# The first half of a ConvFFN's up projection as seven block products, one core of a Trainium2 chip

## What is computed

```
n2 = rmsnorm(h, ln2)
up = n2 @ w_up                                  # 1024 -> 2 * 2816
u, vv = up[..., :D_FF], up[..., D_FF:]
uc, conv_tail = causal_dwconv(u, conv_prev, conv_w, conv_b)   # width 3, along the tokens
h = h + (jax.nn.gelu(uc, approximate=False) * vv) @ w_down
```

## Time and profile before

| | us |
|---|---|
| median of three runs | 832.52 (831.88 to 833.23) |
| span of the profiled execution (first to last instruction) | 830.1 |
| around the span, by the median | 2.4 |
| TensorE busy | 818.1 |
| VectorE busy | 589.9 |
| ScalarE busy | 374.6 |
| GpSimd busy | 219.3 |

### The profile page before, as it was taken

One profiled execution on the slowest core, in us unless ns is written; L12 is line 12 of the kernel. 1 busy time (PEld: TensorE's weight loads), 2 busy tenths in 40 slices (PEclk: granted clock), 3 DMA queues, 4 the chain that ended last, 5 costly groups with the idle time before them and its releaser, 6 DMA issues.

```text
span 830.1 us, 15732 instructions
## 1 busy us (share of the span) xinstructions
PE 818.1 (99%) x6538; PEld 807.0 (97%) x6538; DVE 589.9 (71%) x764; ACT 374.6 (45%) x523; POOL 219.3 (26%) x258
## 2 busy tenths in 40 slices
PE   9999999999999999999999999999999999999996
PEld 8999999999999999999999999999999999999996
DVE  4474668477898886767558877777777756878973
ACT  5553234232354553534343644444444424544574
POOL 4018236434335600000430433333233222000020
PEclk9999999999999999999999999999999999999998
DMA  8769967983324984538899598589699873555522
GB/s 267 219 203 166 269 218 165 193 229 131 108 103 93 208 258 143 164 103 262 147 250 280 88 257 216 157 190 195 248 208 209 222 168 123 180 180 171 175 65 107
DMA packets 167889, 152.27 MB, mean 183 GB/s; under 512 B 6677, under 2 KB 155881, under 8 KB 167804
## 3 DMA queue, kind: packets, MB, share of 16 engines
q1 hardware_dynamic: 121612, 109.73, 42.3%
q0 software_dynamic: 46048, 41.04, 28.9%
q10 hardware_dynamic: 160, 0.53, 0.2%
HBM read 145.31 MB, written 58.40 MB: 245 GB/s over the span
## 4 chain that ended last, share of the span: by engine, by line
PE 92%; DVE 5%; ACT 1%; issue 1%; DMA 0%; DVEq 0%; SPq 0%; ACTq 0%
PE mm L1999 52%; PE ax L2290 14%; PE mm L2404 8%; PE ax L2404 6%; PE ax L2018 6%; PE mm L2290 4%; PE ax L2023 2%; DVE grs L1431 1%; DVE wlo L1421 1%; PE mm L2011 0%; DVE s0g L1588 0%; DVE ylo L1666 0%; PE mm L2018 0%; DVE wlo L1678 0%; ACT whi L1008 0%
## 5 line engine op out<-in xcount | busy, mean ns | idle before, releaser
L1999 PE MATMUL mm<-nhi,whi 128*128 128x272 f32 x960 | 203.2, 293 | 1.2 <-DVE wlo L1421 0.6
L1999 PE MATMUL mm<-nhi,wlo 128*128 128x272 f32 x960 | 199.3, 289 | 0.0
L1999 PE MATMUL mm<-nlo,whi 128*128 128x272 f32 x960 | 198.7, 288 | 0.0
L1008 ACT ACTIVATE whi<-raw 128x1024 fp32r<-128x1024 f32 (+2 forms) x111 | 128.4, 1190 | 67.5 <-PE mm L1999 38.5
L1999 PEld LDWEIGHTS mm<-nhi,whi 128*128 128x128 f32 x960 | 151.9, 189 | 3.8 <-DVE wlo L1421 0.8
L1999 PEld LDWEIGHTS mm<-nlo,whi 128*128 128x128 f32 x960 | 151.3, 189 | 0.0
L1999 PEld LDWEIGHTS mm<-nhi,wlo 128*128 128x128 f32 x960 | 150.8, 190 | 0.0
L1678 DVE TENSOR_TENSOR wlo<-raw,whi 128x1024 fp32r<-128x1024 f32 (+1 forms) x78 | 84.4, 1123 | 5.7 <-ACT whi L1008 3.2
L1421 DVE TENSOR_TENSOR wlo<-raw,whi 128x2048 fp32r<-128x2048 f32 x28 | 67.0, 2394 | 17.8 <-ACT whi L1008 17.8
L939 POOL DMA_DIRECT2D v_sums<-in_w_up x24 | 30.7, 4231 | 117.4 <-DVE mlo L1749 116.6
L1008 ACT ACTIVATE whi<-ring 128x1408 fp32r<-128x1408 f32 x25 | 34.6, 1383 | 44.1 <-PE ax L2404 24.0
(11 more groups left out here) (382 smaller groups left out, 1959.1 us busy)
## 6 DMA issues: line engine op xcount, KB each, us to landing
raw<-in_w_in SPq DMA_DIRECT2D x36, 512.0 KB, 4.6
raw<-in_w_up SPq DMA_DIRECT2D x36, 512.0 KB, 8.2
ring<-w_sums SPq DMA_DIRECT2D x16, 704.0 KB, 4.1
w_sums<-in_w_down SPq DMA_DIRECT2D x12, 704.0 KB, 11.1
w_sums<-in_w_down POOLq DMA_DIRECT2D x12, 704.0 KB, 11.4
ring<-in_w_down SPq DMA_DIRECT2D x9, 704.0 KB, 4.5
v_sums<-in_w_up SPq DMA_DIRECT2D x24, 256.0 KB, 6.8
v_sums<-in_w_up POOLq DMA_DIRECT2D x24, 256.0 KB, 14.6
```

The source lines that it names most:

```text
L1008: return act.activation(out, in_, func, **kw).then_inc(done, 1)
L1999: ins = pe.matmul(mm[:, 2 * j + a, 0:HALF], w, x[:, kx, HALF * a:HALF * (a + 1)], start=first and n == 0 and m == 0, stop=last and n == le ...
```

## The change

u of the pairs 1 to 7 is now done like v, as a unit four and a unit three with seven products, into the banks of mm (GATE_BLOCKS + 14 + 1 = 21 blocks). The weight sums for it come from a new DRAM tensor u_sums: SP copies 21 blocks of 256 KB behind the loads of the two first gate units (14 and 7), and POOL adds. v's sums use the same functions. POOL's transfers are paced by lo_ready over the gates: G_3 and G_1 of u, then G_2 of both; G_4 of both still after m_lo. Blocks now alternate between mm and ax, so a block's products wait for the block before last.

The sum of u's block stands in gact's rows of the next pair. There is no drain of mm by DVE any more: POOL multiplies these rows by rstd into ext (a multiplication of 512 and one of 32 columns for each tile), and there are two ext tiles. The orders of ACT and DVE are rewritten in functions for four kinds of pairs: first_pair, blocked_pair (1 to 7), half_blocked_pair (8) and plain_pair (9, 10). In a blocked pair DVE's low parts of the next two units are put between its additions; the taps of the first tile stand after u's last addition, those of the second after v's first.

```diff
@@ units and blocks
+U_BLOCKS, V_BLOCKS = range(1, 8), range(1, 9)
 UPS = []
 for _i in range(KF // 2):
-    UPS += [("u", _i)] + ([("four", _i), ("three", _i)] if 1 <= _i <= 8 else [("v", _i)])
+    UPS += [("four", 1, _i), ("three", 1, _i)] if _i in U_BLOCKS else [("u", None, _i)]
+    UPS += [("four", 0, _i), ("three", 0, _i)] if _i in V_BLOCKS else [("v", None, _i)]
@@ SP, behind the gate units' loads
+                for i, block in gs_copies[:2] if g == 0 else gs_copies[2:]:
+                    for n in U_BLOCKS:
+                        sp.dma_start(up_sum(0, i, n), up_weights(0, *block, n)).then_inc(us_begun[i], 16)
@@ POOL, the sums
+        for i in U_BLOCKS:
+            pool.wait_ge(lo_ready, U_BLOCK + i)
+            up_weight_sum(0, G_3, i, up_weights(0, 0, 1, i))
+            up_weight_sum(0, G_1, i, up_weights(0, 1, 1, i))
...
+        for i in V_BLOCKS:
+            pool.wait_ge(lo_ready, U_BLOCK + 8 + i // 2)
+            up_weight_sum(1, G_2, i, up_weights(1, 1, 1, i))
...
         pool.wait_ge(m_lo, KD)
...
+        for i in U_BLOCKS:
+            up_weight_sum(0, G_4, i, up_sum(0, G_2, i))
+        for i in V_BLOCKS:
+            up_weight_sum(1, G_4, i, up_sum(1, G_2, i))
@@ POOL, in a pair
+                if i in U_BLOCKS:
+                    out = gact[:, 2 * i + 2 + j, :]
+                    pool.wait_ge(block_added, 4 * u_block(i) + 3 + j)
+                    pool.tensor_tensor(ext_of(t)[:, 2:2 + SEQ], out[:, 0:SEQ], rstd[:, 0:SEQ], ALU.mult).then_inc(ext_prompt, 1)
+                    pool.tensor_tensor(seqs_of(t)[:, :, 2:2 + DEC_SEQ],
...
@@ ACT
+        def blocked_pair(i):
+
+            x, bu, bv = up_unit(i), u_block(i), v_block(i)
+            keep(gact[:, 2 * i + 2, HALVES[0]], mm, bu, 0)
+            keep(gact[:, 2 * i + 3, HALVES[1]], mm, bu, 1)
+            act.wait_ge(block_added, 4 * (bu - 1))
+            keep(u_sum_kept[:, :], mm, bu, 2)
+            next_hi(x)
+            next_hi(x + 1)
+            keep(gact[:, 2 * i, HALVES[0]], ax, bv, 0)
+            first_tap(i, 0)
+            keep(gact[:, 2 * i + 1, HALVES[1]], ax, bv, 1)
+            act.wait_ge(block_added, 4 * bu)
+            keep(v_sum_kept[:, :], ax, bv, 2)
+            gelu(i, 0)
+            first_tap(i, 1)
+            next_hi(x + 2)
+            gelu(i, 1)
+            down_high(i)
+            next_hi(x + 3)
@@ DVE
+        def first_pair():
+
+            x = up_unit(0)
+            extend(0, 0)
+            extend(0, 1)
+            make_sums(usum, V_LN2, 3)
+            taps(0, 0)
+            next_lo(x)
+            t_low(usum, ulow, uhigh, 0)
+            t_low(usum, ulow, uhigh, 1)
+            taps(0, 1)
+            gated(0, 0)
+            down_low(0)
+            t_low(usum, ulow, uhigh, 2)
+            t_low(usum, ulow, uhigh, 3)
+            gated(0, 1)
+            next_lo(x + 1)
+
+        def blocked_pair(i):
+
+            x, bu, bv = up_unit(i), u_block(i), v_block(i)
+            uo, vo = gact_rows(i + 1), gact_rows(i)
+            fourth_product(1, bu, uo, u_sum_kept)
+            lo_piece(x + 2, 0)
+            fifth_product(1, bu, uo, u_sum_kept)
+            sixth_product(1, bu, uo)
+            lo_piece(x + 2, 1)
+            seventh_product(1, bu, uo, u_sum_kept)
+            next_lo(x + 1)
+            taps(i, 0)
+            fourth_product(0, bv, vo, v_sum_kept)
+            taps(i, 1)
+            fifth_product(0, bv, vo, v_sum_kept)
+            lo_piece(x + 4, 0)
+            sixth_product(0, bv, vo)
+            lo_piece(x + 4, 1)
+            gated(i, 0)
+            down_low(i)
+            seventh_product(0, bv, vo, v_sum_kept)
+            gated(i, 1)
+            next_lo(x + 3)
@@ PE
+            b, banks = (u_block(i), mm) if half else (v_block(i), ax)
+            if kind == "four":
+                if i == 1 and half:
+                    for j in range(2):
+                        pe.wait_ge(drained[j], up_fills(j, 1))
...
```

417 lines of the change are left out of this document (258 added, 159 removed).

## The result

The changed kernel takes 881.57 us (median of 4 runs, 878.62 to 886.25) where the kernel before takes 832.88 in the same measurement: a ratio of 1.0595, 95% interval 1.0573 to 1.0618. The direction was forecast, the size was not: +48.7 us against a forecast of +35.5. The time lies at the very end of the range: the ratio 1.0595 on the 832.52 us of the forecast is 882.1, for an upper end of 882.

The account below looks back on a forecast made before the run. The prediction took TensorE to be the bound, busy 818.1 of 830.1 us. Its terms, -10.5 + 4.7 + 40 + 1.5 = +35.7, gave a span of 865.8 and, with 2.4 around it, 868 us; range 843 to 882.

Parts of the forecast that it names:

- The gain: Up projection on TensorE: seven units of 96 matmuls become seven of 84, 10.5 us less, all on the chain.
- The queue walk: Each changed pair, loads in time: 1.1 us late before four(u), 2.6 before its third product, 3.7 together.
- The exclusion of VectorE and POOL: In a pair, VectorE operations with two SBUF inputs, low parts included, and POOL's operations exclude each other: 20.3 of 21.1 us.
- The loads: four(v)'s load lands after 9.1 us, a pair 6.5 over, or 4.3, 3.7 over; 5.7 taken, 40 us for seven.
- Pair 0: Start of pair 1: four(u) waits for VectorE's gating of the second slot, behind new low parts; 4.7 us, bounds 0.9 and 5.5.
- Ahead of the up projection: New copies and accumulations on SP's and POOL's queues, a POOL wait lengthened: 1.5 us, bounds 0 and 8.
- the clock rival: TensorE's clock falls in the new gaps, once per pair, 1.6 us each: adds 11 us, 879 us; chance 0.10.
- The faster case: POOL's new work and the loads fit in the pairs; only pair 0 and 1.5 us remain: 828 us; chance 0.10.
- The second rival: In the pairs, loads land in time and only the queues bind: +21.7 us, 854 us; chance 0.27.

Follow-up runs that it names:

- Run b: The changed kernel without the w_down sums (no copies or accumulations of w_sums; the down projection reads plain blocks): 864.31 us, ratio 1.0389.
- the shortest version: The changed kernel without transfers for u's and w_down's sums, pair 0 reordered, ACT's and VectorE's queues in the last order, POOL's new multiply kept: 834.72 us, ratio 1.0033.
- Run c: The changed kernel without any transfer that makes u_sums (u's blocks read v's sums): 865.73 us, ratio 1.0406.
- run r: The changed kernel without transfers for u's and w_down's sums and without POOL's new multiply, pair 0 and the queues reordered: 831.67 us, ratio 1.0001.
- k_spread: The changed kernel with the w_down sums' transfers issued one at a time at more places, same bytes: 867.59 us, ratio 1.0428.
- a: The changed kernel with ACT's keeps of u's and v's first products moved ahead of high parts: 882.66 us, ratio 1.0609.
- h: The changed kernel with pair 0 alone reordered on VectorE, ACT and TensorE, nothing left out: 880.06 us, ratio 1.0571.

## Why the prediction was wrong, and where it was right

- **The gain**, -10.5 us: 84 matmuls less are in the page, and no run contradicts it.
- **The queue walk**, 3.7 us a pair with loads in time: the places were right, both of them. Run b shows them alone at 0.37 ahead of four(u) (forecast 1.1) and 1.95 ahead of the third product (forecast 2.6), and the pair at 23.8 - 21.1 = 2.7 us over. A little too much, by the same 0.7 at both places.
- **The exclusion of VectorE and POOL.** The forecast took it to hold for low parts, which no row before showed. It does: 2.24 us for a pair of 512 pieces and 2.02 for a piece of 1024 that otherwise takes 1.22. The rule of the Trainium skill (SBUF — State Buffer, Who interferes with whom) names just this pairing, and the trace agrees. Its price in the time, as far as the new multiply goes, is small: 2 us in the changed kernel, which is within the noise, and 3 in the shortest version, since another wait stood beside it. What POOL's older scaling of the Gelu costs by it was not tried.
- **The loads.** The forecast had 5.7 us a pair by a load 9.1 us late. A pair is measured 26.7 - 21.1 = 5.6 over, 2.9 of it by the loads (26.7 - 23.8 in run b) where the forecast had 5.7 - 3.7 = 2.0. Waits make only 27.8/7 = 4.0 of the 5.6; the longer ones bring the clock down besides, which with the gaps named above is the other 1.6. The sum of the pairs, +28.7, meets the forecast's 40 - 10.5 = 29.5 by two errors that cancel: the queues were set 1.0 us a pair too high and the loads 0.9 too low, the clock, kept as a rival of its own, being part of what late loads cost. That this term came out close is luck.
- **Pair 0**: forecast 4.7, measured 5.86 and its clock. The mechanism, the second gating behind the low parts, is as described.
- **Ahead of the up projection: the step that failed.** The prediction looked at SP's queue and at one wait of POOL's, took 1.5 us, and then wrote that POOL's other transfers "are paced over units with no POOL work", costed at nothing, covered by the o projection. That POOL has time for them was true and beside the point. They share the DMA engines with the loads of the gates stage, whose landing time was 5.3 to 5.5 us and had no room for 9 to 10. Run c puts their price at 15.8 us; its trace shows 14 of these at the start of pair 1, waits and their clock. So the term that the prediction put at 1.5 us, transfers included, measured some 14. This is what the forecast lacked: 21.2 us came about ahead of pair 1 against 6.2 forecast, 15 us too little. It gave the bound of 8 for POOL's wait, not for the loads. The measured time stands so near the range's upper end because that end had been set for the clock rival, not because this term was in it.
- **Behind the changed pairs**: forecast 0, measured 4.4, by a load for pair 9 that took 13.34 us behind transfers of w_sums, on the chain above. The prediction did not look beyond pair 8.
- **The clock.** The prediction priced one fall a pair, as a rival, at 11 us. It was there in fact, and not as an alternative: read in windows of 2 us, the grant falls to 0.50 behind eight of the waits between 362 and 720 us. That takes away 17 us of clock in all, of which 3.3 fall while PE waits.
- **The rivals.** The faster case is refuted more strongly than was argued: no slack in ACT's queue was its objection, and run r shows that even with the transfers and the new multiply left out it would be level. The second rival, queues only, is run b's shape of the pair.

Not settled: how the DMA engines share their time between a load and a burst. The prediction held the rule of the Trainium skill (DMA: Bandwidth & Descriptors, Queues, rings and completion order) against the trace: with true turns loads would pass the accumulations quickly. The loads nearly doubled their landing time beside them, and k_spread shows that the number issued together or their place matters. No run varied the packets, so which part is the queue and which the share was not tried.

## What to carry to other kernels

A transfer "in the background" is free only where every load beside it can land late by as much as the burst is long: for each place, set the landing time against the time until the load's first use, and spread them (14 of 17 us came back by that alone, with the same bytes). When a change shortens the cycle of the bound engine, walk every written queue through the new cycle, at its real durations, before counting the gain: here 1.5 us a pair saved met 2.7 us of queue lateness as the order was written, and 1.7 in the best order found. Undoing one of several waits in series shows nothing (a, h); take the largest out first and then test the others.

## What the runs showed of the hardware that was not expected

- TensorE's granted clock falls with the long waits: 0.83, 0.73, 0.84 and 0.85 in the 10 us stretches with waits of 4.0 to 5.9 us, so that a third to a half of such a stretch ran at 1.2 GHz in place of 2.4. In the changed kernel that is some 14 us beside 45.6 of waiting. The length of a wait alone does not tell where it falls. In the trace of the changed kernel every wait of 3.2 us or more was followed by a fall, but of the shorter ones those of 1.95 us at 544.7, 2.46 at 714.4 and 2.76 at 668.2 were too, and those of 2.68 at 611.5 and 1.95 at 518.7 were not. Run k has four of 2.0 us between 516 and 600 us, all at 1.00.
- An accumulation costs POOL's queue 1.1 to 1.4 us to issue (8.90 for eight, 9.44 for seven), in which POOL computes nothing: a copy of 0.20 us that waited behind eight of them cost PE 2.74 us.
- The two engines' stretch on each other reaches low parts (1.22 to 2.02 us), taps (0.80 to 1.37) and gatings (0.71 to 1.88), and POOL's own multiply of 512 columns, 1.26 us at the shortest and 1.93 on the average of the changed kernel.
